# A two-layer decoder trunk on one core: attention levels decayed in place, gains read from PSUM, four more weight tiles kept in SBUF

## The reference

```python
def peer(h, w_q, k1, k2, u_tab, v_tab):        # per block of 128 positions
    q = (xb @ w_q).reshape(128, 8, 256)         # 8 heads
    ...                                         # top 16 of 128 x 128 product keys per head -> eid, gate
    u_e = jnp.take(u_tab, eid, axis=0)
    act = gelu(einsum('thkd,td->thk', u_e, xb))
    v_e = jnp.take(v_tab, eid, axis=0)
    return einsum('thk,thkd->td', gate * act, v_e)

def mixer_b(h, ...):                            # layer 1
    q, k, v, r, g_lr = split(h @ w_in)
    gc = cumsum(log_sigmoid(g_lr @ w_g2 + b_g) / 16)
    scores[t, s] = sum_k q[t,k] * exp(gc[t,k] - gc[s,k]) * k[s,k]     # s <= t
    o = rmsnorm(scores @ v + carried state, norm_g) * silu(r)
    return o @ w_out
```

## Time and profile before

| | us |
|---|---|
| median of three runs | 1547.35 (1546.37 to 1548.38) |
| the profiled execution, its own time | 1548.85 |
| its span, first to last instruction | 1546.7 |
| busy in the span: PE / DVE / ACT / POOL | 1363.9 / 1064.4 / 655.9 / 599.0 |
| mean granted TensorE clock | 0.965 of 2.4 GHz |
| moved by DMA | 621.99 MB, mean 402 GB/s |

### The profile page before, as it was taken

How to read it: one execution, slowest core, us unless ns; L and a number is a source line. 1 busy time by engine, 2 the same in 40 slices (tenths; PEclk the granted TensorE clock), 3 DMA queues, 4 the chain that set the end, 5 groups by cost and what they waited for, 6 DMA issues and landing times.

```text
span 1546.7 us, 15419 instructions
## 1 busy us (share of the span) xinstructions
PE 1363.9 (88%) x4372; PEld 726.5 (47%) x4372; DVE 1064.4 (69%) x2686; ACT 655.9 (42%) x1720; POOL 599.0 (39%) x540
## 2 busy tenths in 40 slices
PE   9999978889887898979887999989998888887776
PEld 7886534445442454434343654445454445433322
DVE  5688677777677668767665666777676765666675
ACT  5665343333234456534433544554343423333333
POOL 0101444444454433334534323334444444444442
PEclk9999999999999999999999999999999999999999
DMA  7896999999999999999999999999999999999997
GB/s 264 291 356 250 418 421 420 421 421 421 423 416 421 418 422 418 419 422 421 422 418 405 422 423 423 380 422 417 422 406 423 422 422 421 423 420 415 418 421 281
DMA packets 97524, 621.99 MB, mean 402 GB/s; under 512 B 10986, under 2 KB 11130, under 8 KB 31904
## 3 DMA queue, kind: packets, MB, share of 16 engines
q0 software_dynamic: 75552, 542.83, 85.1%
q1 hardware_dynamic: 21744, 77.94, 12.9%
q10 hardware_dynamic: 144, 0.26, 0.0%
HBM read 619.94 MB, written 1.05 MB: 401 GB/s over the span
## 4 chain that ended last, share of the span: by engine, by line
PE 37%; DMA 37%; DVE 18%; issue 4%; ACT 2%; POOL 1%; ACTq 0%; POOLq 0%; SPq 0%; DVEq 0%
PE psum L1471 37%; DMA row<-in_uv,ids 36%; DVE row L1238 7%; POOL row L570 1%; ACT gate_diag L779 1%; DVE look L1166 1%; DVE numbers L1171 1%; ACT diag L789 1%; DMA row<-in_uv,half_ids 1%; DVE look L1169 1%; DVE scores L1097 1%; DVE topi L1094 1%; DVE topi L1105 0%; DVE tile_lo L940 0%; DVE candpos L1105 0%
## 5 line engine op out<-in xcount | busy, mean ns | idle before, releaser
L1471 PE MATMUL psum<-row,diag 128*128 128x512 f32 x1976 | 948.5, 622 | 167.1 <-ACT diag L789 165.6
L570 POOL DMA_INDIRECT row<-in_uv,ids x508 | 579.8, 1141 | 851.7 <-PE psum L1471 740.4
L1238 DVE SCALAR_TENSOR_TENSOR row<-row,hn 128x1024 f32<-128x1024 f32 x512 | 623.7, 1223 | 400.9 <-DMA row<-in_uv,ids 399.9
L1471 PEld LDWEIGHTS psum<-row,diag 128*128 128x128 f32 x1976 | 370.6, 197 | 649.0 <-issue 375.6
L769 ACT ACTIVATE acted<-dots 128x2 f32<-128x2 f32 x256 | 52.1, 203 | 763.1 <-DVE row L1238 762.7
L789 ACT ACTIVATE diag<-gate_diag,acted 128x128 f32<-128x128 f32 x496 | 174.6, 387 | 0.1
L779 ACT ACTIVATE gate_diag<-ident,gate 128x128 f32<-128x128 f32 x496 | 169.0, 386 | 0.8 <-DVE gate L1230 0.8
L940 DVE TENSOR_TENSOR tile_lo<-raw,tile_hi 128x1024 fp32r<-128x1024 f32 x32 | 39.1, 1222 | 27.7 <-ACT tile_hi L615 27.5
L1471 PE MATMUL psum<-raw,hT_mix 128*128 128x512 f32 x120 | 56.4, 592 | 0.0
L1471 PEld LDWEIGHTS psum<-hT_query,raw 128*128 128x128 f32 x416 | 50.3, 192 | 11.0 <-issue 11.0
L1471 PE MATMUL psum<-hT_query,raw 128*128 128x128 f32 x416 | 50.6, 275 | 0.0
(11 more groups left out here) (256 smaller groups left out, 1157.2 us busy)
## 6 DMA issues: line engine op xcount, KB each, us to landing
raw<-in_a_in SPq DMA_DIRECT2D x32, 512.0 KB, 4.7
raw<-in_w_q SPq DMA_DIRECT2D x28, 512.0 KB, 8.5
raw<-in_b_rv SPq DMA_DIRECT2D x27, 512.0 KB, 8.0
raw<-in_b_qk SPq DMA_DIRECT2D x16, 512.0 KB, 8.0
row<-in_uv,ids POOLq DMA_INDIRECT x508, 15.6
aout<-in_a_out SPq DMA_DIRECT2D x13, 512.0 KB, 8.7
early_q<-in_w_q SPq DMA_DIRECT2D x12, 512.0 KB, 9.6
kept<-in_a_out SPq DMA_DIRECT2D x3, 512.0 KB, 15.0
```

What stands on the lines that cost most here:

```text
L570: pool.indirect_dma_start(rows[s][:, :], None, t[f"uv{l}"][:, :], bass.IndirectOffsetOnAxis(ids[:, h, g, k:k + 1], 0)).then_inc(row_loaded ...
L1238: dve.scalar_tensor_tensor(u, u, 1.0, hn[:, h, :], ALU.mult, ALU.mult, accum_out=dots[:, n // TOPK % 2, k:k + 1]).then_inc(dotted, 1)
L1471: return pe.matmul(o, a, b, start=start, stop=stop, skip_group_check=True)
```

## The change

- **Tiles kept.** `b_rv` tiles 5, 9, 11 and 13 join `KEPT` and leave the ring, where each was loaded twice. They are loaded once: tile 5 right behind the early query tiles, tile 13 after the norm of row 31, tile 9 after the use of a query tile at row 77 and tile 11 after one at row 99.
- **Levels in place.** `qe` and `ke` go away. `decayed` multiplies the later side of each block of `ed` by q and the sooner side by k, in place, 256 columns each; the product takes `ed` for both operands; `keep` copies the later rows only. `diff(L)` now waits for the product of level L-2 where it waited for `decayed(L-2)`.
- **Overlays.** `br` and `bo` lie over `gq`, `gk`, `gcum` and `ed1`. The two held query tiles (w_q 12 and 13) move to places 20 and 21. Their loads move two tiles down SP's queue; the first waits for the last level's product (w = 60), the second for the products of `OUT` (w = 65). Their use, head query (0, 6), moves from w = 66 to w = 70 of half 1.
- **Gains.** `spread_gain` rides at w = 96 of both halves and at row 389, and `scale` and the last norm read PSUM. ScalarE's copies go away. GpSimd loads the gain rows at rows 213, 341 and 374 into the first partition of `bo`.
- **The heads' norm gain** is a column: the multiplication L1373 goes away, and ScalarE's two copies of 128x512 behind the turning at w = 75 become eight of 128x128 with a scale.
- **Rings.** `ids` is 2 groups deep, `gate` 4. The keys of layer 1 (128 KiB) are loaded at row 120. The 1/16 moves from the triangle into the copy of `gcum`.

```diff
 MASKS_AT = 120
-GAIN_ROWS = {112: (0, 6), 3 * PICKS - 8: (1, 0)}
...
-KEPT = [("b_out", 2), ("b_out", 3), ("b_out", 4), ("b_rv", 2), ("b_rv", 3), ("b_out", 5), ("b_out", 6), ("b_rv", 4)]
-KEPT_PLACE = (26, 27, 28)
+KEPT = [("b_out", 2), ("b_out", 3), ("b_out", 4), ("b_rv", 2), ("b_rv", 5), ("b_rv", 3), ("b_out", 5), ("b_out", 6),
+        ("b_rv", 9), ("b_rv", 11), ("b_rv", 13), ("b_rv", 4)]
+KEPT_OWN = 5
+KEPT_PLACE = (26, 27, 28, 25, 24)
+KEPT_GAIN = KEPT_OWN + len(KEPT_PLACE)
+KEPT_RAW = KEPT_GAIN + 1
 G_ROWS = 33
-KEPT_LATE = [i for i in range(len(KEPT) - 1) if i != 3]
+KEPT_LATE = (0, 1, 2, KEPT_GAIN, 5, 6, 7, 8)
 WEIGHTS = [w for w in WEIGHTS if w[:2] not in HELD + KEPT]
 PLACE = {w: m for m, w in enumerate(WEIGHTS)}
...
-X_SUMS, X_ROOT, X_TURN = 95, 97, 100
...
+X_SUMS, X_GAIN, X_ROOT, X_TURN = 95, 96, 97, 100
...
+    + [(0, 6, 2 * PICKS + 70), (0, 7, 2 * PICKS + 93)]
     + [(1, 7, 2 * PICKS + 104), (1, 0, 2 * PICKS + 110)] + [(1, 1 + i, 3 * PICKS + 3 + 10 * i) for i in range(6)])
...
         hn = sb("hn", [P, TT, D])
-        gain_row = sb("gain_row", [P, D])
-        ids = sb("ids", [P, TT, P_HEADS, TOPK], U32)
-        gate = sb("gate", [P, TT, P_HEADS, TOPK])
+        (gain_row,) = overlay([("gain_row", [P, D], F32)])
...
             ("k_last", [P, B_HEADS, P], F32),
             ("score_in", [P, B_HEADS, P], F32),
             ("score_x", [P, B_HEADS, P], F32),
             ("bv", [P, TT, D], F32),
         ])
-        (_, br, bo) = overlay([
-            ("pad_decays", [P, ROW_SLOTS * 2 * D + 5 * B_HEADS * P], F32),
-            ("br", [P, D], F32),
-            ("bo", [P, D], F32),
...
+        last_gained = br[:, 0:BANK]
+        z_la, z_tmp = ed0.rearrange("p a b -> p (a b)"), ed1.rearrange("p a b -> p (a b)")
         early_q = [wide(place, f"early_q{j}", [P, TILE]) for j, place in enumerate(EARLY_PLACE)]
-        held_late = [wide(18, "held_q12", [P, TILE]), wide(19, "held_q13", [P, TILE])]
+        held_late = [wide(20, "held_q12", [P, TILE]), wide(21, "held_q13", [P, TILE])]
         kept_wide = [wide(place, f"kept_wide{place}", [P, TILE]) for place in KEPT_PLACE]
         last_wide = wide(29, "last_wide", [P, TILE])
         sb("reserved_wide", [P, 30 * TILE])
         held = [scores[:, 1, 0:P_HEADS, :].rearrange("p a b -> p (a b)"), last_wide, scores[:, 1, P_HEADS:P_ROWS, :].rearrange("p a b -> p (a b)")]
         held += held_late
-        kept = [sb(f"kept{i}", [P, TILE]) for i in range(len(KEPT) - len(KEPT_PLACE) - 1)]
...
         aout += kept[:N_AOUT - len(AOUT_PLACE)]
-        kept += [*kept_wide, raw[RING]]
+        kept += [*kept_wide, kept_gain, raw[RING]]
         masks = sb("masks", [P, B_LEVELS + 1, P], U8)
-        bnorm_row = sb("bnorm_row", [P, B_HV])
...
+            sp.dma_start(kept[4][:, :], t[KEPT[4][0]][KEPT[4][1]]).then_inc(kept_loaded, 16)
             for i in KEPT_LATE:
                 name, c = KEPT[i]
                 if i == 2:
                     sp.wait_ge(sums_done, 2 * TT)
                 elif i < 2:
                     sp.wait_ge(other_used, len(AOUT_PLACE) + i + 1)
+                elif i == KEPT_GAIN:
+                    sp.wait_ge(hn_ready[1], 2 * TT)
                 else:
-                    place = EARLY_PLACE.index(KEPT_PLACE[i - 4]) + RAW_SLOTS
+                    place = EARLY_PLACE.index(KEPT_PLACE[i - KEPT_OWN]) + RAW_SLOTS
                     sp.wait_ge(query_used, QUERIES.index((place, None)) + 1)
                 sp.dma_start(kept[i][:, :], t[name][c]).then_inc(kept_loaded, 16)
             for m, (name, c, h) in enumerate(WEIGHTS):
...
                     sp.wait_ge(query_used, QUERIES.index((RING, 1)) + 1)
-                    sp.dma_start(kept[-1][:, :], t[KEPT[-1][0]][KEPT[-1][1]]).then_inc(kept_loaded, 16)
+                    sp.dma_start(kept[KEPT_RAW][:, :], t[KEPT[KEPT_RAW][0]][KEPT[KEPT_RAW][1]]).then_inc(kept_loaded, 16)
+                    i = KEPT_GAIN - 1
+                    sp.wait_ge(query_used, QUERIES.index((EARLY_PLACE.index(KEPT_PLACE[-1]) + RAW_SLOTS, 1)) + 1)
+                    sp.dma_start(kept[i][:, :], t[KEPT[i][0]][KEPT[i][1]]).then_inc(kept_loaded, 16)
                 if m == PLACE["b_rv", N_BRV - 1, 0]:
                     sp.wait_ge(shifted, P_HEADS + 4)
                     sp.wait_ge(query_used, len(QUERIES))
                     for i in range(2):
                         sp.dma_start(held[i][:, :], t["b_out"][i]).then_inc(held_loaded[HELD_LOADS[i]], 16)
-                if m == PLACE["b_rv", N_BRV - 1, 1]:
-                    sp.wait_ge(qk_decayed, 2 * (B_LEVELS + 1))
-                    for i in (3, 4):
-                        sp.dma_start(held[i][:, :], t["w_q1"][HELD[i][1]]).then_inc(held_loaded[HELD_LOADS[i]], 16)
+                if m == PLACE["b_rv", N_BRV - 1, 1] + 2:
+                    sp.wait_ge(level_done, level_number(1, B_LEVELS + 1))
+                    sp.dma_start(held[3][:, :], t["w_q1"][HELD[3][1]]).then_inc(held_loaded[HELD_LOADS[3]], 16)
...
+            def load_gain_part(i, free, count):
+
+                pool.wait_ge(free, count)
+                pool.dma_start(bo[0:1, :], t["gains"][i:i + 1]).then_inc(gain_part_loaded, 16)
...
-                if n == 3 * TOPK:
-                    load_gain(3, hn_ready[1], 2 * TT)
                 if n == MASKS_AT:
                     pool.wait_ge(query_used, len(QUERIES))
                     pool.dma_start(masks[:, :, :], t["masks"]).then_inc(gla_loaded, 16)
                     pool.wait_ge(scores_done[0], len(QUERIES) // 2)
                     pool.dma_start(w_g2, t["w_g2"]).then_inc(gla_loaded, 16)
+                    pool.dma_start(keysT[:, :, :], t["keysT"][1]).then_inc(gla_loaded, 16)
                     pool.memset(score_in[:, :, :], 0.0).then_inc(score_zeroed, 1)
                 if n == 2 * PICKS + 2 * TOPK:
                     pool.wait_ge(o_done, 1)
                     pool.memset(score_in[:, :, :], 0.0).then_inc(score_zeroed, 1)
+                if n in (PICKS + O_TURN + 12, 2 * PICKS + O_TURN + 12):
+                    load_gain_part(3, o_turned, 2 * (n // PICKS))
                 if n == 3 * PICKS - 10:
-                    load_gain(4, hn_ready[3], 2 * TT)
...
                 if w == O_TURN + 2:
-                    turned(hT_mix, o_turned, oT_ready, 2 * h, 2)
+                    for half in range(2):
+                        act.wait_ge(o_turned, 2 * h + half + 1)
+                        for c in range(4):
+                            ins = act.activation(hT_mix[:, 4 * half + c, :], psum[:, 2 + half, c * P:(c + 1) * P], ACT.Copy, scale=bnorm_col[:, c % 2:c % 2 + 1])
+                        ins.then_inc(oT_ready, 1)
                 if w == X_SUMS:
                     square(3, h)
...
                 after(did(dve.reciprocal(rstd[:, h:h + 1], rms[:, h:h + 1])))
-                if load < len(gain_loaded) - 2:
-                    dve.wait_ge(gain_loaded[load], 16)
+                if bank is None:
+                    dve.wait_ge(gain_loaded, 16)
                 else:
-                    dve.wait_ge(gain_copied, 2 * (load - len(gain_loaded) + 2) + 2)
+                    dve.wait_ge(gain_spread, spreads)
                 for half in range(2):
                     cols = slice(half * BANK, (half + 1) * BANK)
-                    dve.scalar_tensor_tensor(hn[:, h, cols], x[:, h, cols], rstd[:, h:h + 1], gain_row[:, cols],
+                    gains = gain_row[:, cols] if bank is None else psum[:, bank + half, :]
+                    dve.scalar_tensor_tensor(hn[:, h, cols], x[:, h, cols], rstd[:, h:h + 1], gains,
                                              ALU.mult, ALU.mult).then_inc(hn_ready[i], 1)
...
+                dve.wait_ge(gain_spread, 6)
+                dve.tensor_tensor(last_gained, x[:, 1, BANK:D], psum[:, 5, :], ALU.mult).then_inc(gain_applied, 1)
                 dve.wait_ge(rms_ready[4], TT)
                 dve.reciprocal(rstd[:, 1:2], rms[:, 1:2]).then_inc(rstd_ready, 1)
                 dve.wait_ge(rstd_ready, 2)
-                dve.scalar_tensor_tensor(hn[:, 1, 0:BANK], x[:, 1, 0:BANK], rstd[:, 1:2], gain_row[:, 0:BANK],
+                dve.scalar_tensor_tensor(hn[:, 1, 0:BANK], x[:, 1, 0:BANK], rstd[:, 1:2], psum[:, 4, :],
                                          ALU.mult, ALU.mult).then_inc(hn_ready[4], 1)
...
             def diff(h, L):
 
-                if L >= 3:
-                    dve.wait_ge(qk_decayed, (B_LEVELS + 1) * h + L - 2)
+                if L == 3 and h == 0:
+                    dve.wait_ge(qk_decayed, 1)
+                elif L >= 3:
...
             def decayed(h, L):
+                e = ed[L % 2]
                 dve.wait_ge(decay_ready, (B_LEVELS + 1) * h + L)
                 dve.wait_ge(qk_copied, 2 * B_HEADS * (h + 1))
                 if L == 1:
                     if h == 0:
-                        dve.tensor_tensor(k_last[:, :, :], gk[:, :, :], ed[1][:, :, :], ALU.mult).then_inc(qk_decayed, 1)
```

(40 more changed lines are left out.)

122 lines of the change are left out of this document (54 added, 68 removed).

## The result

| | before | after |
|---|---|---|
| median of the runs, us | 1547.12 (1546.37 to 1548.38, 4 runs) | 1526.03 (1525.44 to 1527.95, 4 runs) |
| ratio, 95% interval | | 0.9866 [0.9854, 0.9878] |
| span of the profiled execution, us | 1546.7 | 1523.7 |
| mean granted clock, of 2.4 GHz | 0.965 | 0.977 |
| moved by DMA | 621.99 MB, mean 402 GB/s | 619.79 MB, mean 407 GB/s |

The kernel became faster by 21.1 us. The prediction was 1546.2 us with a range down to 1542.2: far outside.

The account below looks back on a forecast made before the run. The prediction took full DMA engines as the bound from about 150 us, with TensorE setting the pace in half 1. Terms +5.3 - 4.4 - 2.1 = -1.2 us took 1547.35 to 1546.15, say 1546.2 us; range 1542.2 to 1549.4.

Parts of the forecast that it names:

- a tile of 0.524 MB costs 0.524 MB / 420 GB/s: Where DMAs are full, from about 150 us on, every byte costs time: 1.25 us for each tile.
- At nothing: Parts priced at no cost: `diff`'s new wait, `scale` from PSUM, row 389's spread, small loads, removed copies, rings of `ids` and `gate`.
- So in half 1 a tile not loaded between 976 and 1150 us is not worth its transfer: Layer 1, second half: TensorE frees row slots too slowly, so dropping a load there does not save its 1.25 us.
- Transfers alone count: Rival for the whole kernel: every stretch follows the bytes moved, -4.7 us, 1542.6 us; chance 0.27.
- Layer 0: Four added tile loads at +5.0 us and the moved keys at +0.3, nothing hiding them: +5.3 us.
- Half 0: First half of layer 1: four loads go, limited by how far TensorE can follow: -4.4 us, between -3.4 and -5.0.
- Half 1: Second half of layer 1: TensorE's own path counts, to w = 109 and 110: -2.1 us, between -2.9 and +1.0.
- no slack is left in them: Gathers of w = 109 and 110 in half 1 landed 11.8 and 12.8 us after issue, taken as leaving no reserve.
- The Trainium skill's rule on weight loads: Weight-load share measures TensorE's headroom; at 30.09 of 60.30 us TensorE has room, so -4.7 us would hold.
- Gating: Gating of r in both halves loses a 1.23 us VectorE multiplication that stands on the chain: -1.2 us each.
- The held tile at w = 70: Half 1: second held query tile, loaded behind w = 65, makes TensorE wait 0 to 1.8 us, taken as +0.5.
- The gap ahead of w = 100: Half 1: TensorE's idle 2.91 us for a diagonal is used up because rows land earlier: -2.9 us.

Follow-up runs that it names:

- after_rows_off128: Kernel after with a 128-byte pad ahead of the row slots, which begin at byte 83072: 1543.25 us, ratio 0.9972.
- after_rows_off256: Kernel after with a pad of 64 elements ahead of the row slots, which begin at byte 83200, 256 past a multiple of 512: 1526.47 us, ratio 0.9858.
- before_rows_aligned: Kernel before with an unused 384-byte pad ahead of the row slots, which begin at byte 86016 instead of 85632: 1531.15 us, ratio 0.9889.
- after_four_in_ring: Kernel after with `b_rv` tiles 5, 9, 11 and 13 loaded twice through the ring again and not kept: 1530.92 us, ratio 0.9891.
- the single dose: Kernel after with the products of levels 5 and 7 taken three times over in half 1, 3.6 us more TensorE work: 1525.95 us, ratio 0.9856.
- the double dose: Kernel after with the products of levels 4 to 7 taken three times over in half 1, 7.1 us more TensorE work: 1530.84 us, ratio 0.9886.

## Why the prediction was wrong

**The step that failed first: "a tile of 0.524 MB costs 0.524 MB / 420 GB/s", with the rate taken as fixed, and the rings of `ids` and `gate` under "At nothing".** The rings add no wait, as I wrote, but they and the smaller keys move the row slots by 2688 bytes and so change the price of every byte of 542.70 MB. By the medians of after_rows_off128 and after that is 17.2 us (16.4 by the ratios); of my miss of 20.2 us (1546.2 to 1526.0) it is all but 3. I had listed what each edit adds, removes and makes wait, and never what lies behind it in the buffer. A sum from the records agrees: 512 rows of 128 packets on 16 engines are 4096 packets each, and 4.5 ns less for each makes 18.4 us; over all such packets of the two traces the mean falls from 315.7 to 311.8 ns, which makes 16.0. Why a packet is longer off the boundary no run here shows. The nearest rule is the Trainium skill's (DMA: Bandwidth & Descriptors, How a descriptor splits into AXI transactions; my expectation of after_rows_off256 named the section before it): a transaction that reads must start at a 256-byte-aligned address, so a descriptor that doesn't start at one begins at the boundary below it and also fetches bytes that it doesn't use. It is told of reads, and here it is the place of the written end that was varied; the offsets of 0, 64, 128 and 256 bytes agree with a boundary of 256, but 64 bytes past it cost as much as 128 (1543.57 and 1543.25 us), so the number of bytes below the start is not the price.

**The step that failed second: "So in half 1 a tile not loaded between 976 and 1150 us is not worth its transfer".** With the slots 128 bytes off as they were, the change gives 1543.25 us, ratio 0.9972 [0.9961, 0.9983]: 2.6 to 6.0 us faster. My sum said 1.2; the rival "Transfers alone count" said 4.7 (1542.6 us), and it was right on what the change was meant to do. Step by step, after beside before_rows_aligned:

- Layer 0: predicted +5.3, measured +4.7 (4.1 to 7.3 over seven traces). Right.
- Half 0: predicted -4.4 (-3.4 to -5.0), measured -5.2 (-4.4 to -5.2 over those traces), and the windows were full at 425 GB/s. The limits that I put on it, 1.42 us of idle time and 2.0 from VectorE, did not bind: 3.6 us of added TensorE work cost nothing there.
- Half 1: predicted -2.1 (to -2.9), measured -4.3 (-4.1 to -5.4 over those traces), of it 3.7 by the tiles alone. This term was wrong in kind. TensorE without a gap for 60.52 us and 332 GB/s were true readings, and after has both again: 58.86 us in its chain of waits, 349 GB/s in 15 us. But neither says that an end is late, since a gather that is issued later also waits less in the queue. I took 11.8 us for the shortest landing and wrote "no slack is left in them"; 10.3, 6.8 and 6.3 us followed. What I took for the floor was the queue at that moment, not the transfer.
- The trace of before had it already. The gather issued at 238.1 us landed after 8.0 us, with the DMAs full at 420 GB/s between 232 and 240 us:

```profile
DMA to landing us min/median/max: 8.0/8.0/8.0
```

  And the two gathers issued behind the 60.52 us of unbroken TensorE work, at 1036.3 and 1038.9 us, took 19.9 us, where those issued between 300 and 350 us took 14.7: the queue was long, not short, where I said that TensorE was late.

```profile
row<-in_uv,ids POOLq DMA_INDIRECT x2, 19.9
```

- The Trainium skill's rule on weight loads as TensorE's headroom (Perfetto Trace Analysis, Identifying the Most-Contended Engine), which stood beside the rival, agrees with the result: a share of 44.08 of 100 us between 928 and 1028, and room for 3.6 us of added products.
- Gating: -1.2 at the stall, measured 4.93 against 3.67 us. Right as a stall, worth 0.6 at the end by the medians, 0.3 by the traces, and not 2.4.
- The held tile at w = 70: predicted a wait of +0.5, measured 0.16. ScalarE's eight copies (near 1060 us): predicted +0.4, measured nothing, since the chain runs on TensorE from 1059.12 for 61.52 us without a break. The gap ahead of w = 100: predicted -2.9, but idle time of 3.68 us by w = 104 shows that TensorE now waits for rows and dots there, which is what a path set by transfers looks like.
- At nothing: `diff`'s wait, `scale` from PSUM, GpSimd's small loads. after_four_in_ring and before_rows_aligned differ by 0.2 us, so all of it together is nothing that these runs can tell.

What stays open: after the single dose the DMAs had moved some 1.2 MB less than in after at 1450 us (the trace's records), worth 2.8 us at 426 GB/s, and yet the rows there were only 0.6 us later. A mean rate over 16 engines hides how far single engines are ahead; whether that is it was not tried. Nor is all of the double dose accounted for: 7.1 us less the 4.0 that the landing gave up (10.3 to 6.3) leave 3.1, and half 1 grew by 4.2.

## What to carry to other kernels

List not only what an edit computes, loads and waits for, but also which buffers it moves: after any change in sizes, look where the destination of the largest transfers begins, and try it on a multiple of 256 bytes. Compare the rate in a stretch that the edit doesn't touch first; if it differs, the cause is global. An engine without gaps and a dip in the DMA rate are no proof of a bound while the time from issue to landing is above its shortest, and the shortest is to be looked for in the whole trace; add a few us of harmless work to that engine and see whether the end moves.
